# All transposes of an expert visit in one group behind its gate and up products, and the next rows loaded ahead of the last result's store

## The chip, the cores and the metric

One core of a Trainium2 chip runs the whole program. The metric is the device time of one execution in microseconds; the time before is the median of three runs.

## The reference, cut to what is computed

Two decoder layers over 256 positions of width 1024, float32. Layer 0 is a stick-breaking attention with a dense SwiGLU, layer 1 a latent attention (MLA) with a SwiGLU of 8 experts, of which each position takes its best two. The change lies in the experts:

```python
logits = (h @ w_router).astype(jnp.float32) + b_router.astype(jnp.float32)
top_vals, top_idx = lax.top_k(logits, TOP_K)          # TOP_K = 2
top_w = jax.nn.softmax(top_vals, axis=-1)
gates = jnp.sum(jax.nn.one_hot(top_idx, N_EXPERTS, dtype=jnp.float32) * top_w[..., None], axis=-2)
out = jnp.zeros_like(h)
for e in range(N_EXPERTS):                            # 8 experts, 1408 hidden columns each
    out = out + gates[..., e:e + 1] * _swiglu(h, w_gu[e], w_down[e])
```

with `_swiglu(h, w_gu, w_down)` = `(silu(a) * b) @ w_down`, where `a` and `b` are the halves of `h @ w_gu`.

## The kernel before

**Numbers in two parts.** Every product is made of three: each float32 operand is split into a high part that TensorE takes as it is (`F32R`) and a low part, the difference. The product is hi x hi + lo x hi + hi x lo. ScalarE copies a weight piece out of the ring into `m_hi` (`ehi`, L950), VectorE subtracts into `m_lo` (`elo`, L1608). The same is done with activations: `xe_hi`/`xe_lo`, `eT_hi`/`eT_lo`.

**The weight stream.** The sync engine (SP) loads the weights in pieces of at most 1 MB into a ring of six buffers and waits for `freed`, which VectorE counts up with every split, before it fills a buffer again. `m_hi` and `m_lo` have three buffers each (`NB`), so `ehi(k)` waits until TensorE has finished piece k - 3 (`used`).

**A visit.** The positions chosen for an expert are gathered as 128 rows of `x_rows` in DRAM; a visit handles 128 rows of one expert. Here there are 8 visits: the loop `Fori(0, last)` runs seven times with `more=True`, and the last visit is written out behind it with `more=False`. A visit has 18 pieces: 12 of gate and up in three groups j = 0, 1, 2 of 4 pieces (512, 512 and 384 hidden columns, `EW = (4, 4, 3)` blocks of 128), and 6 of the down product, `down(a, g)`, for the output halves a = 0, 1 and the groups g = 0, 1, 2. The gate product of group j is in PSUM bank 2j, the up product in bank 2j + 1, the down products in banks 6 and 7.

**Between gate/up and down.** For each group: ScalarE's `sil(j)` (L1024) takes the Silu of the gate into `esil`; VectorE's `times_up(j)` (L1700) multiplies it with the up product into `ehid[j % 2]`, counted in `e_hid`; TensorE's `turn(j)` (L2386 to L2391) transposes its 4, 4 or 3 blocks with the identity into bank 2j; ScalarE's `eg_hi(j)` (L1028) copies that into `eT_hi`, VectorE's `eg_lo(j)` (L1707) writes the difference to `eT_lo` and counts `e_glo`, for which `down(0, g)` waits. These pieces of work are sewn into the weight splits by hand, in the order that the functions of each engine give.

**Where the transposes stand.** On TensorE, `turn(0)` and `turn(1)` stand in the middle of the gate and up pieces of the following group, `turn(2)` behind `down(0, 0)`. The next visit's input is transposed in two halves, `turn_x` (L2330, four transposes each), behind `down(0, 1)` and `down(0, 2)`, into banks 1 and 3. ScalarE's `x_half` (L997) scales and shifts them into `xe32` and copies to `xe_hi`, VectorE's `x_lo` makes `xe_lo`. The last visit has `turn_sel` (two transposes of the selection matrix) instead.

**The rows in and out.** ScalarE's `y_out` at the start of visit i copies the finished banks 6 and 7 to `ysb` (`e_y`). The GpSimd queue then stores `ysb` to `y_rows`, waits until the store has landed (`s_y`), waits until the last `xe_in` has been transposed (`e_xT`), and loads the next 128 rows into `xe_in` (`s_xe`), L566 to L571. TensorE waits for `s_xe` ahead of its first `turn_x`. So `ysb` is free for the next `y_out` since TensorE got through `s_xe`.

Of the kernel before, what the change touches and what calls it, by code (L numbers as in the profile page):

```python
# [28 lines left out]
P = 128  # L29
# [41 lines left out]
def trunk(nc, x_d, c_d, pos_d, ada_w, ada_b, norm_g, sb_w_in, sb_w_out, mla_w_in, mla_g_q, mla_w_q_up,  # L71
# [83 lines left out]
    with ctx:  # L155
# [137 lines left out]
        eT_hi = sb("eT_hi", [P, EFC, P], F32R, at=base + 20480)  # L293
        eT_lo = sb("eT_lo", [P, EFC, P], F32R, at=base + 26624)
        esil = [sb(f"esil{b}", [P, 512], at=base + 32256 + 2048 * b) for b in range(2)]
        ehid = [sb(f"ehid{b}", [P, 512], at=base + 36352 + 2048 * b) for b in range(2)]
        xT32 = sb("xT32", [P, TC, DC, P], at=base + 36864)
        above = sb("above", [P, TC, E, E], at=acc_at)
        level = sb("level", [P, TC, E, E], at=acc_at + 512)
# [187 lines left out]
        def _(pool):  # L487
# [76 lines left out]
            pool.wait_ge(visit_ok, 1)  # L564
            last = pool.value_load(n_last[0:1, 0:1], min_val=E - 1, max_val=2 * E - 1)
            with pool.Fori(0, last) as i:  # L566
                pool.wait_ge(e_y, i + 1)
                pool.dma_start(y_rows.rearrange("(v p) n -> v p n", p=P)[i], ysb[:, :]).then_inc(s_y, 16)
                pool.wait_ge(s_y, 16 * i + 16)
                pool.wait_ge(e_xT, 2 * i + 2)  # L570
                pool.dma_start(xe_in[:, :], x_rows.rearrange("(v p) n -> v p n", p=P)[i + 1]).then_inc(s_xe, 16)  # L571
            pool.wait_ge(e_y, last + 1)
            pool.dma_start(y_rows.rearrange("(v p) n -> v p n", p=P)[last], ysb[:, :]).then_inc(s_ylast, 16)
            pool.wait_ge(row_ok, 2)
# [12 lines left out]
        def _(act):  # L587
# [431 lines left out]
            def visit_hi(i, more):  # L1019
                def sil(j):  # L1020
                    act.wait_ge(used, M0 + 4 * j + 4 + NK * i)
                    if j >= 2:
                        act.wait_ge(e_hid, EG * i + j - 1)
                    act.activation(esil[j % 2][:, 0:gw[j]], ps[:, 2 * j, 0:gw[j]], ACT.Silu).then_inc(e_sil, 1)  # L1024

                def eg_hi(j):
                    act.wait_ge(e_hidT, EG * i + j + 1)
                    act.activation(eT_hi[:, f0[j]:f0[j] + EW[j], :].rearrange("p a b -> p (a b)"),  # L1028
                                   ps[:, 2 * j, 0:gw[j]], ACT.Copy).then_inc(e_ghi, 1)

                y_out(M0 + NK * i)
                for j in range(EG):
                    ehi(i, 4 * j + 3)
                    if j >= 1:
                        eg_hi(j - 1)
                    ehi(i, 4 * j + 4)
                    ehi(i, 4 * j + 5)
                    sil(j)
                    ehi(i, 4 * j + 6)
                if more:  # L1040
                    eg_hi(EG - 1)
                    ehi(i, NG + 3)
                    x_half(2 * i + 2, 0)
                    ehi(i, NG + 4)
                    ehi(i, NG + 5)
                    ehi(i, NK)
                    x_half(2 * i + 2, 1)
                    for k in range(1, NB):
                        ehi(i, NK + k)
# [13 lines left out]
            with act.Fori(0, last) as i:  # L1063
                visit_hi(i, True)
            visit_hi(last, False)
            act.wait_ge(e_hidT, EG * last + EG)
            act.activation(eT_hi[:, f0[EG - 1]:EFC, :].rearrange("p a b -> p (a b)"),
                           ps[:, 2 * EG - 2, 0:gw[EG - 1]], ACT.Copy).then_inc(e_ghi, 1)
            act.wait_ge(sel_mm, 1)
            act.activation(selT[:, :], ps[:, 1, 0:T], ACT.Copy).then_inc(selT_ok, 1)  # L1070
            act.wait_ge(wt_all, 1)
# [36 lines left out]
        def _(dve):  # L1108
# [588 lines left out]
            def visit_lo(i, more):  # L1697
                def times_up(j):
                    dve.wait_ge(e_sil, EG * i + j + 1)
                    dve.tensor_tensor(ehid[j % 2][:, 0:gw[j]], esil[j % 2][:, 0:gw[j]], ps[:, 2 * j + 1, 0:gw[j]],  # L1700
                                      ALU.mult).then_inc(e_hid, 1)

                def eg_lo(j):
# [4 lines left out]

                for j in range(EG):
                    elo(i, 4 * j + 3)  # L1710
                    if j >= 1:
                        eg_lo(j - 1)
                    elo(i, 4 * j + 4)
                    if j == EG - 1:
                        times_up(j)
                        elo(i, 4 * j + 5)
                        eg_lo(j)
                    else:
                        elo(i, 4 * j + 5)
                        times_up(j)  # L1720
# [67 lines left out]
        def _(pe):  # L1788
# [557 lines left out]
            def visit(i, more):  # L2346
# [39 lines left out]
                def turn(j):  # L2386
                    pe.wait_ge(e_hid, EG * i + j + 1)
                    for a in range(EW[j]):
                        ins = pe.transpose(ps[:, 2 * j, a * P:(a + 1) * P], ehid[j % 2][:, a * P:(a + 1) * P],
                                           ident[:, :])  # L2390
                    ins.then_inc(e_hidT, 1)  # L2391

                pe.wait_ge(e_xhi, 2 * i + 1)
                for j in range(EG):
                    gate_up(4 * j)
                    gate_up(4 * j + 1)
                    if j == 0:
                        pe.wait_ge(e_xlo, 2 * i + 2)
                    if j >= 1:
                        turn(j - 1)  # L2400
                    gate_up(4 * j + 2)
                    gate_up(4 * j + 3)
                pe.wait_ge(e_y, i + 1)
                for g in range(EG):
                    pe.wait_ge(e_glo, EG * i + g + 1)
                    down(0, g)
                    if g == 0:
                        turn(EG - 1)
                        if not more:
                            turn_sel()  # L2410
                    elif more:
                        if g == 1:
                            pe.wait_ge(s_xe, 16 * i + 16)
                        turn_x(2 * i + 2, g - 1)
                for g in range(EG):
                    down(1, g)
                    if g == 1 and not more:
# [82 lines left out]
```

## Time and profile before

| | |
|---|---|
| median of 3 runs | 819.75 us (819.63 to 819.96) |
| the profiled execution | 819.59 us, its span 817.8 us |
| TensorE, matmuls | 794.6 us busy, 97% of the span |
| TensorE, weight loads | 707.0 us, 86% |
| VectorE | 693.9 us, 85% |
| ScalarE | 542.4 us, 66% |
| GpSimd | 48.3 us, 6% |
| chain that ended last | 81% TensorE, 6% VectorE, 4% DMA, 3% ScalarE |
| DMA | 284.31 MB, mean 348 GB/s |

A profile row of the order of time has the start in us from the start of the span, the duration in us of the whole row (from its first start to its last end), the engine (PE is TensorE's matmuls, PEld its weight loads, DVE is VectorE, ACT is ScalarE, POOL is GpSimd), the line of the kernel, what was written and read, and `xN` for N instructions in a row. Matmuls overlap: the one that follows starts before the last has ended, so their cost is the distance between starts and not the duration. A bracket at the end gives how long the engine was idle before the row and who released it.

### The profile page before, as it was taken

The numbers are of one execution on the slowest core, as the hardware profiler recorded it, in microseconds if no ns is written. First come the engines' busy times: TensorE is split into PE (matmuls) and PEld (weight loads), VectorE is DVE, ScalarE is ACT, GpSimd is POOL, SyncE is SP. The second block draws the span as 40 slices with busy tenths as digits, with TensorE's granted clock in tenths as the row PEclk, the third lists the DMA queues.
The fourth block names the chain that finished last, engine by engine and source line by source line (L and its number), as shares of the span: only waits on it lengthen the run. The fifth ranks groups of instructions, "written<-read, shape, count | busy, mean of one in ns | idle before, by whom it ended". The sixth has DMA issues, their size and how long they took to land.

```text
span 817.8 us, 12488 instructions
## 1 busy us (share of the span) xinstructions
PE 794.6 (97%) x4678; PEld 707.0 (86%) x4678; DVE 693.9 (85%) x587; ACT 542.4 (66%) x575; POOL 48.3 (6%) x54
## 2 busy tenths in 40 slices
PE   4999999999999999999999999999999999999995
PEld 4999778999999888999888888888888888888884
DVE  4998797889989886878479898988989898898998
ACT  5447846534344334667388797978788797878875
POOL 1000020020000300000011000000000000000120
PEclk9999999999999999999999999999999999999998
DMA  8999676599999997399929999999999999999992
GB/s 336 422 423 374 247 285 233 187 372 344 357 380 399 355 366 277 132 382 421 421 66 392 426 391 416 351 425 363 399 406 355 412 350 427 359 403 400 359 413 80
DMA packets 46793, 284.31 MB, mean 348 GB/s; under 512 B 6028, under 2 KB 6031, under 8 KB 21156
## 3 DMA queue, kind: packets, MB, share of 16 engines
q1 hardware_dynamic: 41002, 269.06, 83.8%
q0 software_dynamic: 3584, 12.60, 4.0%
q10 hardware_dynamic: 2170, 2.13, 0.8%
q8 instruction: 26, 0.43, 0.2%
q14 instruction: 11, 0.09, 0.0%
HBM read 258.09 MB, written 25.17 MB: 346 GB/s over the span
## 4 chain that ended last, share of the span: by engine, by line
PE 81%; DVE 6%; issue 4%; DMA 4%; ACT 3%; POOL 1%; SPq 0%; DVEq 0%; ACTq 0%; POOLq 0%
PE ps L2367 9%; PE ps L2363 8%; PE ps L2362 8%; PE ps L1855 7%; PE ps L1863 7%; PE ps L1859 7%; PE ps L2378 4%; PE ps L2379 4%; PE ps L2383 4%; PE ps L1791 3%; PE ps L1793 3%; PE ps L1792 3%; DMA ring<-in_ada_w 2%; DVE w_lo L1119 2%; PE ps L1810 1%
## 5 line engine op out<-in xcount | busy, mean ns | idle before, releaser
L1611 DVE TENSOR_TENSOR w_lo<-ring,w_hi 128x2048 fp32r<-128x2048 f32 (+1 forms) x96 | 210.0, 2200 | 29.7 <-ACT w_hi L954 29.4
L608 ACT ACTIVATE w_hi<-ring 128x2048 fp32r<-128x2048 f32 (+1 forms) x56 | 106.4, 1901 | 136.3 <-PE ps L1863 79.9
L954 ACT ACTIVATE w_hi<-ring 128x2048 fp32r<-128x2048 f32 (+1 forms) x96 | 174.8, 1839 | 8.8 <-PE ps L2367 8.8
L1119 DVE TENSOR_TENSOR w_lo<-ring,w_hi 128x2048 fp32r<-128x2048 f32 (+1 forms) x56 | 131.5, 2350 | 33.2 <-ACT w_hi L608 32.7
L1855 PE MATMUL ps<-hT_hi,w_hi 128*128 128x256 f32 x480 | 117.1, 280 | 0.2 <-ACT hT_hi L710 0.2
L1863 PE MATMUL ps<-hT_hi,w_lo 128*128 128x256 f32 x480 | 116.7, 279 | 0.0
L1859 PE MATMUL ps<-hT_lo,w_hi 128*128 128x256 f32 x480 | 116.5, 279 | 0.0
L1611 DVE TENSOR_TENSOR m_lo<-ring,m_hi 128x1536 fp32r<-128x1536 f32 (+1 forms) x48 | 92.7, 1930 | 2.3 <-ACT m_hi L954 1.9
L2363 PE MATMUL ps<-w_hi,xe_lo 128*128 128x512 f32 (+1 forms) x256 | 92.3, 376 | 0.0
L2362 PE MATMUL ps<-w_hi,xe_hi 128*128 128x512 f32 (+1 forms) x224 | 85.1, 380 | 0.0
L1855 PEld LDWEIGHTS ps<-hT_hi,w_hi 128*128 128x128 f32 x480 | 82.5, 188 | 0.5 <-issue 0.4
L1863 PEld LDWEIGHTS ps<-hT_hi,w_lo 128*128 128x128 f32 x480 | 82.6, 188 | 0.0
L1859 PEld LDWEIGHTS ps<-hT_lo,w_hi 128*128 128x128 f32 x480 | 82.4, 187 | 0.0
L954 ACT ACTIVATE m_hi<-ring 128x1536 fp32r<-128x1536 f32 (+1 forms) x48 | 78.0, 1624 | 6.6 <-PE ps L2367 5.6
L1138 DVE SCALAR_TENSOR_TENSOR acc<-ring,cond,acc 128x2048 f32<-128x2048 f32 x28 | 67.4, 2408 | 0.9
L2367 PE MATMUL ps<-w_lo,xe_hi 128*128 128x512 f32 (+1 forms) x256 | 65.2, 376 | 0.1
L2363 PEld LDWEIGHTS ps<-w_hi,xe_lo 128*128 128x128 f32 x256 | 48.1, 188 | 7.3
L2367 PEld LDWEIGHTS ps<-w_lo,xe_hi 128*128 128x128 f32 x256 | 47.2, 188 | 8.1 <-DVE w_lo L1611 0.5
L2378 PE MATMUL ps<-w_hi,eT_hi 128*128 128x512 f32 x128 | 51.4, 402 | 0.0
L2379 PE MATMUL ps<-w_hi,eT_lo 128*128 128x512 f32 x128 | 50.1, 392 | 0.0
L2362 PEld LDWEIGHTS ps<-w_hi,xe_hi 128*128 128x128 f32 x224 | 42.1, 188 | 6.0
L2363 PE MATMUL ps<-m_hi,xe_lo 128*128 128x384 f32 (+1 forms) x128 | 46.5, 363 | 0.0
(407 smaller groups left out, 1464.6 us busy)
## 6 DMA issues: line engine op xcount, KB each, us to landing
ring<-in_moe_w_gu SPq DMA_DIRECT2D x64, 1024.0 KB, 6.7
ring<-in_ada_w SPq DMA_DIRECT2D x48, 1024.0 KB, 7.1
ring<-in_moe_w_down SPq DMA_DIRECT2D x32, 1024.0 KB, 7.4
ring<-in_moe_w_gu SPq DMA_DIRECT2D x32, 768.0 KB, 7.9
ring<-in_ffn_w_gu SPq DMA_DIRECT2D x22, 1024.0 KB, 6.1
ring<-in_sb_w_in SPq DMA_DIRECT2D x12, 1024.0 KB, 9.2
ring<-in_moe_w_down SPq DMA_DIRECT2D x16, 768.0 KB, 6.7
ring<-in_ffn_w_down SPq DMA_DIRECT2D x11, 1024.0 KB, 7.2
```

Of the source, the lines that this page charges most:

```text
L608: act.activation(split_of(m)[0][:, 0:cols_n], ring[n % R][:, 0:cols_n], ACT.Copy).then_inc(hi_done, 1)
L954: act.activation(m_hi[k % NB][:, 0:n_c], ring[(N0 + k) % R][:, 0:n_c], ACT.Copy).then_inc(hi_done, 1)
L1119: dve.tensor_tensor(split_of(m)[1][:, 0:cols_n], ring[n % R][:, 0:cols_n], split_of(m)[0][:, 0:cols_n].bitcast(F32), ALU.subtract).then_in ...
L1611: dve.tensor_tensor(m_lo[k % NB][:, 0:n_c], ring[(N0 + k) % R][:, 0:n_c], m_hi[k % NB][:, 0:n_c].bitcast(F32), ALU.subtract).then_inc(free ...
L1855: return pe.matmul(at(f), bh[:, k, f * P:(f + 1) * P], hT_hi[:, k0 + k, :], start=(begin and k == 0 and f % 2 == 0), stop=False, skip_grou ...
L1859: return pe.matmul(at(f), bh[:, k, f * P:(f + 1) * P], hT_lo[:, k0 + k, :], start=False, stop=stop, skip_group_check=True)
L1863: return pe.matmul(at(f), bl[:, k, f * P:(f + 1) * P], hT_hi[:, k0 + k, :], start=False, stop=stop, skip_group_check=True)
L2362: pe.matmul(o, xe_hi[:, 2 * q + h, :], bh[:, h, s, :], start=q + h == 0, stop=False)
L2363: pe.matmul(o, xe_lo[:, 2 * q + h, :], bh[:, h, s, :], start=False, stop=False)
L2367: ins = pe.matmul(ps[:, 2 * j + s, 0:gw[j]], xe_hi[:, 2 * q + h, :], bl[:, h, s, :], start=False, stop=q == 3 and h == 1)
L2378: pe.matmul(o, eT_hi[:, f, :], bh[:, h, :], start=f == 0, stop=False)
L2379: pe.matmul(o, eT_lo[:, f, :], bh[:, h, :], start=False, stop=False)
```

## The change

On TensorE `turn(0)`, `turn(1)` and `turn(2)` leave their places; behind the last gate and up piece there now stand `turn(0)`, `turn(1)`, the two `turn_x` of the next visit (in the last visit `turn_sel`), and `turn(2)`, and then all down products. For that `ehid` gets a third buffer. ScalarE and VectorE have their three `eg_hi` and `eg_lo` behind `sil(2)` and `times_up(2)`. The GpSimd queue issues the load of the next rows first and the store behind it, and waits for the store no more; TensorE does, ahead of `down(1, 0)`.

```diff
-        ehid = [sb(f"ehid{b}", [P, 512], at=base + 36352 + 2048 * b) for b in range(2)]
+        ehid = [sb(f"ehid{b}", [P, 512], at=base + 36352 + 2048 * b) for b in range(EG)]
...
             with pool.Fori(0, last) as i:
+                pool.wait_ge(e_xT, 2 * i + 2)
+                pool.dma_start(xe_in[:, :], x_rows.rearrange("(v p) n -> v p n", p=P)[i + 1]).then_inc(s_xe, 16)
                 pool.wait_ge(e_y, i + 1)
                 pool.dma_start(y_rows.rearrange("(v p) n -> v p n", p=P)[i], ysb[:, :]).then_inc(s_y, 16)
-                pool.wait_ge(s_y, 16 * i + 16)
-                pool.wait_ge(e_xT, 2 * i + 2)
-                pool.dma_start(xe_in[:, :], x_rows.rearrange("(v p) n -> v p n", p=P)[i + 1]).then_inc(s_xe, 16)
...
                 for j in range(EG):
                     ehi(i, 4 * j + 3)
-                    if j >= 1:
-                        eg_hi(j - 1)
                     ehi(i, 4 * j + 4)
                     ehi(i, 4 * j + 5)
                     sil(j)
+                    if j == EG - 1:
+                        for n in range(EG):
+                            eg_hi(n)
                     ehi(i, 4 * j + 6)
                 if more:
-                    eg_hi(EG - 1)
                     ehi(i, NG + 3)
...
             visit_hi(last, False)
-            act.wait_ge(e_hidT, EG * last + EG)
-            act.activation(eT_hi[:, f0[EG - 1]:EFC, :].rearrange("p a b -> p (a b)"),
-                           ps[:, 2 * EG - 2, 0:gw[EG - 1]], ACT.Copy).then_inc(e_ghi, 1)
...
-                    dve.tensor_tensor(ehid[j % 2][:, 0:gw[j]], esil[j % 2][:, 0:gw[j]], ps[:, 2 * j + 1, 0:gw[j]],
+                    dve.tensor_tensor(ehid[j][:, 0:gw[j]], esil[j % 2][:, 0:gw[j]], ps[:, 2 * j + 1, 0:gw[j]],
...
                 for j in range(EG):
                     elo(i, 4 * j + 3)
-                    if j >= 1:
-                        eg_lo(j - 1)
                     elo(i, 4 * j + 4)
                     if j == EG - 1:
                         times_up(j)
+                        for n in range(EG - 1):
+                            eg_lo(n)
                         elo(i, 4 * j + 5)
                         eg_lo(j)
...
                     gate_up(4 * j + 1)
                     if j == 0:
                         pe.wait_ge(e_xlo, 2 * i + 2)
-                    if j >= 1:
-                        turn(j - 1)
                     gate_up(4 * j + 2)
                     gate_up(4 * j + 3)
+                for j in range(EG - 1):
+                    turn(j)
+                if more:
+                    pe.wait_ge(s_xe, 16 * i + 16)
+                    for b in range(2):
+                        turn_x(2 * i + 2, b)
+                else:
+                    turn_sel()
+                turn(EG - 1)
                 pe.wait_ge(e_y, i + 1)
                 for g in range(EG):
                     pe.wait_ge(e_glo, EG * i + g + 1)
                     down(0, g)
-                    if g == 0:
-                        turn(EG - 1)
-                        if not more:
-                            turn_sel()
-                    elif more:
-                        if g == 1:
-                            pe.wait_ge(s_xe, 16 * i + 16)
-                        turn_x(2 * i + 2, g - 1)
+                if more:
+                    pe.wait_ge(s_y, 16 * i + 16)
                 for g in range(EG):
                     down(1, g)
```

## Rows read from the trace of the kernel before

**Rows 1.** Stretches: us, busy PE, PEld, DVE, ACT, POOL (instructions), granted clock, DMA share, GB/s

```profile
570.30:617.69 47.39, 47.39 (x231) 40.62 (x229) 42.15 (x27) 38.85 (x36) 1.08 (x2) 1.00 0.97 387
15.00:18.00 3.00, 3.00 (x29) 3.00 (x29) 2.86 (x3) 0.60 (x2) 0.00 (x0) 1.00 1.00 419
```

**Rows 2.** Who waited for whom, 440 to 818 us: total us, times, longest

```profile
ACT eT_hi L1028 <- PE ps L2389: 26.8, 23, 1.2
...
POOL xe_in L571 <- DMA y_rows<-ysb: 54.3, 6, 9.3
```

**Rows 3.** Instructions of L2389 and of L2334: count, ns min/median/max, first and last start

```profile
L2389 PE MATMUL ps<-ident,ehid x88: 270/272/275, 444.5 to 793.8; 128*128 128x128 f32 x88
...
L2334 PE MATMUL ps<-ident,xe_in x56: 270/272/275, 465.1 to 752.1; 128*128 128x128 f32 x56
```

**Rows 4.** PE in order of time, visit from 570.3: the pieces' hi x lo matmuls

```profile
582.99 1.07 PE L2367 MATMUL ps<-w_lo,xe_hi 128*128 128x512 f32 x4
...
585.71 1.07 PE L2367 MATMUL ps<-m_lo,xe_hi 128*128 128x512 f32 x4
...
588.92 1.08 PE L2367 MATMUL ps<-w_lo,xe_hi 128*128 128x512 f32 x4
...
596.05 0.86 PE L2367 MATMUL ps<-w_lo,xe_hi 128*128 128x384 f32 x4
...
598.57 0.85 PE L2367 MATMUL ps<-w_lo,xe_hi 128*128 128x384 f32 x4
...
600.65 0.85 PE L2367 MATMUL ps<-m_lo,xe_hi 128*128 128x384 f32 x4
...
603.20 1.08 PE L2383 MATMUL ps<-w_lo,eT_hi 128*128 128x512 f32 x4
...
606.30 1.08 PE L2383 MATMUL ps<-w_lo,eT_hi 128*128 128x512 f32 x4
...
609.04 0.86 PE L2383 MATMUL ps<-m_lo,eT_hi 128*128 128x512 f32 x3
...
612.02 1.07 PE L2383 MATMUL ps<-w_lo,eT_hi 128*128 128x512 f32 x4
```

**Rows 5.** PE in order of time: 16 transposes in a row, layer 0

```profile
15.21 1.91 PE L1918 MATMUL ps<-ident,xhat 128*128 128x128 f32 x16
```

**Rows 6.** PE in order of time, last visit: around turn(2) and turn_sel

```profile
792.66 1.08 PE L2383 MATMUL ps<-w_lo,eT_hi 128*128 128x512 f32 x4
...
795.98 1.07 PE L2383 MATMUL ps<-w_lo,eT_hi 128*128 128x512 f32 x4
```

**Rows 7.** All engines in order of time: turn(1) and what follows; the end of gate/up

```profile
596.74 0.60 PE L2389 MATMUL ps<-ident,ehid 128*128 128x128 f32 x4
...
597.38 0.60 ACT L1028 ACTIVATE eT_hi<-ps 128x512 fp32r<-128x512 f32 x1 [1.03 <-PE ps L2389]
...
598.11 0.68 DVE L1707 TENSOR_TENSOR eT_lo<-ps,eT_hi 128x512 fp32r<-128x512 f32 x1
...
601.54 0.49 ACT L1024 ACTIVATE esil<-ps 128x384 f32<-128x384 f32 x1
...
601.93 1.48 ACT L954 ACTIVATE m_hi<-ring 128x1536 fp32r<-128x1536 f32 x1
...
602.07 0.56 DVE L1700 TENSOR_TENSOR ehid<-esil,ps 128x384 f32<-128x384 f32 x1
```

**Rows 8.** All engines in order of time, tail: TensorE released by ACT and by DVE

```profile
807.52 0.60 ACT L1061 ACTIVATE yl_hi<-ps 128x512 fp32r<-128x512 f32 x1
...
808.26 0.70 PE L2426 MATMUL ps<-yl_hi,selT 128*128 128x512 f32 x2 [0.78 <-ACT yl_hi L1061]
808.43 0.68 DVE L1738 TENSOR_TENSOR yl_lo<-ps,yl_hi 128x512 fp32r<-128x512 f32 x1
...
809.17 0.73 PE L2426 MATMUL ps<-yl_lo,selT 128*128 128x512 f32 x2 [0.21 <-DVE yl_lo L1738]
```

**Rows 9.** POOL in order of time, the same visit: the load of the next rows

```profile
584.57 0.54 POOL L571 DMA_DIRECT2D xe_in<-x_rows  x1 [9.13 <-DMA y_rows<-ysb]
```

More of the change, by code:

```diff
@@ L2388, in turn @@
                     for a in range(EW[j]):
-                        ins = pe.transpose(ps[:, 2 * j, a * P:(a + 1) * P], ehid[j % 2][:, a * P:(a + 1) * P],
+                        ins = pe.transpose(ps[:, 2 * j, a * P:(a + 1) * P], ehid[j][:, a * P:(a + 1) * P],
                                            ident[:, :])
```

## The prediction

> **What bounds the kernel now.** I read the busy shares by stretch first, then the list of waits, then TensorE in order of time. In one expert visit TensorE is busy for 47.39 of 47.39 us, with a granted clock of 1.00, the 16 DMA engines for 0.97 of the time, VectorE for 42.15 and ScalarE for 38.85 us [rows 1]. TensorE is in none of the visits' large waits; those that touch the change are ScalarE's, 26.8 us in 23 waits for the transposes of the hidden rows, and the GpSimd queue's, 54.3 us for the store of the last result [rows 2]. Both are idle time of engines that are not the bound. So only what changes TensorE's own sequence can count. There are 8 visits: 88 transposes at L2389 are 8 x 11, and 56 at L2334 are 7 x 8, since the last visit loads no next rows [rows 3].
>
> **What the transposes cost today.** A piece of 12 matmuls with 512 columns takes 585.71 - 582.99 = 2.72 us, one with 384 columns 600.65 - 598.57 = 2.08, so a matmul 0.227 or 0.173 [rows 4]. The same stretches with a group in them [rows 4]: 588.92 - 585.71 = 3.21, so turn(0) costs 0.49; 598.57 - 596.05 = 2.52, turn(1) 0.44; 606.30 - 603.20 = 3.10, turn(2) 0.38 (three transposes); 609.04 - 606.30 = 2.74 less 10 matmuls, the first half of the next rows 0.47; 612.02 - 609.04 = 2.98 less 11 matmuls, the second half 0.49. Sum: 2.27 us a visit for 19 transposes in five groups. In a long train 16 transposes take 1.91 us, the last of which stands for 0.27, so the pitch is 1.64/15 = 0.109 us [rows 5] and 19 of them are 2.07. The five groups have an overhead of 2.27 - 2.07 = 0.20 us, 0.04 to 0.05 each. That is all that grouping can take off TensorE: four fifths of it, 0.16 a visit, or 0.20 if all goes. The last visit has 11 transposes and two of `sel` in three groups: its first two as above (0.49 and 0.44), the third 795.98 - 792.66 = 3.32 less 2.72 = 0.60 [rows 6]; sum 1.53.
>
> **What the change adds: a chain at the boundary.** Before, the halves of `eT` for group 0 were ready long before the down product; turn(2) even ran behind down(0, 0). Now down(0, 0) waits for turn(0), ScalarE's copy and VectorE's difference, and all of these stand behind the end of gate and up. I count from the moment when TensorE could start the next matmul, 600.65 + 4 x 0.173 = 601.34 [rows 4]. ScalarE starts its Silu at 601.54 (+0.20) and its next work at 601.93 (+0.59); a copy of turned data starts 597.38 - 596.74 = 0.64 after the first transpose of its group. So eg_hi(0) runs from +0.64 for 0.60, to +1.24 [rows 7]. VectorE takes up ScalarE's result 0.04 later (601.54 + 0.49 to 602.07), so at +1.28; but its product for group 2 starts at +0.73 and takes 0.56, to +1.29. eg_lo(0), 0.68, ends at +1.97 [rows 7]. The hand-over to a waiting TensorE is in the trace twice, in the tail: 0.06 us after VectorE (809.11 to 809.17) and 0.14 after ScalarE (808.12 to 808.26); the first matmul after the wait is followed 0.70 - 0.39 = 0.31 later instead of 0.23, so a restart costs 0.08 [rows 8]. Down(0, 0) starts at +2.03 to +2.11. TensorE's own train needs +2.07 to that point, so the wait is nearly hidden; what hides it are the 8 transposes of the next rows, and turn(2) finds its input (+1.29) before its turn at +1.74.
>
> I take +2.11 and one group's overhead, 0.05: 2.16 a visit against 2.27, a gain of 0.11, times 7 visits 0.77 us. In the last visit the 8 transposes are missing, so the cover is thinner: 13 transposes are 1.42, the chain still ends at +2.11, and 2.16 stands against 1.53, a loss of 0.63. It falls in the part from which everything follows to the end. **Sum: -0.14 us.** The profiled execution took 819.59 us (span 817.8 plus 1.8 around it), the median of the runs is 819.75, 0.16 above it; so I forecast 819.6.
>
> **What is moved and costs nothing.**
> - VectorE behind the boundary: after eg_lo(1) its next split (piece 13, 2.29 at the most) runs from about +2.5 to +4.8. Down(0, 1) asks for it 20 matmuls after +2.11, at +6.6. eg_lo(2) then ends at +5.3 and the split of piece 14 at +7.1, asked for at +2.11 + 24 x 0.227 + 6 x 0.227 = +8.9. ScalarE's copy of piece 15 must now wait for down(0, 0), +2.11 + 2.72 + 0.2 = +5.0; it is wanted at +9.6. If this cover were gone, TensorE would wait here in the middle of the down product.
> - The load of the next rows: it moves from behind the store to ahead of it, so that it starts a visit earlier. At present it starts at 584.57, after 9.13 us behind the store [rows 9], and TensorE reads it from 607 on. It wasn't late; the earlier start is worth nothing, but without it the transposes couldn't stand at the boundary (+0.9 is 602). On the GpSimd queue the store stands behind the wait for the transposes of the rows before, which were done in the visit before. Same bytes, same count of DMAs.
> - The store's wait moves to TensorE, ahead of down(1, 0). The store is out by 584.57 - 9.13 = 575.4 and done by 584.6 [rows 9]; down(1, 0) of that visit starts at 612.02 + 4 x 0.227 = 612.9 [rows 4], 28 us later. What would queue behind this wait is all of TensorE.
> - Third buffer for `ehid`, and the copy after the loop taken into the visit: no instruction more. ScalarE's 26.8 us of waits [rows 2] mostly go; nothing waited for them.
>
> **A rule against the change.** Across 16 transposes in a row the granted clock stays 1.00 in the trace [rows 1, 5]. The Trainium skill, "TensorE: Matmul & The Clock Gate", part 4, says that transposes in PE mode don't count as busy for the clock gate. By that rule a train of 19 with a wait behind it could cost clock.
>
> **Rivals.**
> 1. *The boundary wait is dearer than the tail's hand-over* (slower). Now the head of TensorE's queue waits in every visit, with five waits in the train, and the next weight load can't run ahead. It decides from 0.2 us more a visit: 8 x 0.2 on top of 819.6 is 821.2; at 0.25 it is 821.6. For it: the two hand-overs differ by 0.08 already, and the chain has three engines in it. Against: none of the hand-overs read is above 0.14. 0.17.
> 2. *The whole overhead goes* and something with it. Bound by the train alone: 7 x 0.20 = 1.4 off, 2.07 - 1.53 = 0.54 on, 818.9. Should the slow pitch of down(0, 0) (603.20 - 600.65 - 0.69 = 1.86 for 8 matmuls instead of 1.81, [rows 4]) go too, 0.04 x 8 = 0.3 more: 818.6. Only beyond that would it be faster by what can be told. 0.10 for such a result.
> 3. *The clock falls.* A stretch as long as the train, 2.1 us, at 1.2 instead of 2.4 GHz would cost about 2.1 us more each visit, 17 in all: 836. Rows show no fall, and the wait behind the train is short. 0.01.
> 4. *The change does nothing it says*: no group is shorter for standing beside another, since the 0.20 us may belong to the first matmuls after any change of width (down(0, 0) shows 0.04 with no transpose before it). Then a visit pays 2.27 and the chain's +2.11 is covered: 0 for 7 visits, the last one 2.27 - 1.53 = 0.7 on: 820.5. It lies within the 0.72 of no change that can be told.
>
> **Numbers.** Forecast as computed, 0.72, its own range 818.7 to 820.5 (from 7 x 0.20 gained, to rival 4). A change can be told from about 0.2%, 1.6 us. For 8 in 10 I take 818.4, rival 2 and the scatter of the runs, to 821.3, rival 1 at its deciding point. Faster 0.10, same 0.72, slower 0.18.
>
> **What the profile after would show.** TensorE with one train of 19 transposes behind each last gate and up piece, and the first down matmul 2.0 to 2.2 us after it; four stretches of 2.72, 2.08 and 2.72 us where groups were; the visit at about 47.3 instead of 47.39 us; the last visit longer by about 0.6. ScalarE's wait of 26.8 us for transposes down to some 5. Wrong: a wait of TensorE for `eT_lo` of over 0.2 us a visit, a wait of any product in the down part for a split, or a granted clock below 1.00.

## The result: slower by a quarter of a per cent, and the profile after

| | before | after |
|---|---|---|
| median of 10 runs | 819.75 us (819.63 to 820.04) | 821.81 us (821.13 to 822.36) |
| ratio | | 1.0025, interval 1.0017 to 1.0032 |
| profiled execution, its span | 819.59, 817.8 us | 821.46, 819.7 us |

The change costs 2.06 us, outside the range given (818.4 to 821.3), and the runs scatter over 1.2 us where they scattered over 0.4.

The busy times of the page after; no instruction was added or removed on a compute engine, and VectorE's time is the same to a tenth:

```profile
span 819.7 us, 12466 instructions
...
PE 796.5 (97%) x4678; PEld 709.4 (87%) x4678; DVE 693.9 (85%) x587; ACT 544.5 (66%) x575; POOL 46.3 (6%) x54
```

Where the 1.9 us of span went shows in the distances from the first gate matmul of a visit (L2355 before, L2351 after) to that of the next. Three rows of each kernel: its first, second and last visit. Before, TensorE in order of time:

```profile
427.68 1.19 PE L2355 MATMUL ps<-w_hi,xe_hi 128*128 128x512 f32 x4
...
475.57 1.07 PE L2355 MATMUL ps<-w_hi,xe_hi 128*128 128x512 f32 x4
...
759.77 1.07 PE L2355 MATMUL ps<-w_hi,xe_hi 128*128 128x512 f32 x4
```

and after:

```profile
427.93 1.19 PE L2351 MATMUL ps<-w_hi,xe_hi 128*128 128x512 f32 x4
...
476.51 1.07 PE L2351 MATMUL ps<-w_hi,xe_hi 128*128 128x512 f32 x4
...
761.09 1.07 PE L2351 MATMUL ps<-w_hi,xe_hi 128*128 128x512 f32 x4
```

| | before | after | difference | forecast |
|---|---|---|---|---|
| up to the first visit | 427.68 | 427.93 | +0.25 | 0 |
| first visit | 47.89 | 48.58 | +0.69 | -0.11 |
| the six in the middle, each | 47.37 | 47.43 | +0.06, six times 0.38 | -0.11, -0.66 |
| last visit to the end of the span | 58.0 | 58.6 | +0.6 | +0.63 |

The 0.25 us lie ahead of everything that the change touches: one execution's scatter (in the thirteen traces of this document the first visit starts anywhere from 427.54 to 428.36). The last row looks as forecast, but two things are in it, of which one hides part of the other; see below. The same table, made from one execution of each kernel, carries most of what follows; "middle" is the mean of the six.

**The boundary after**, in a middle visit, all engines in order of time (weight loads left out but for one):

```profile
600.77 0.86 PE L2363 MATMUL ps<-m_lo,xe_hi 128*128 128x384 f32 x4
...
601.46 1.04 PE L2385 MATMUL ps<-ident,ehid 128*128 128x128 f32 x8
601.74 0.49 ACT L1023 ACTIVATE esil<-ps 128x384 f32<-128x384 f32 x1 [0.24 <-PE ps L2363]
602.13 1.08 ACT L1027 ACTIVATE eT_hi<-ps 128x512 fp32r<-128x512 f32 x2
...
602.27 0.55 DVE L1696 TENSOR_TENSOR ehid<-esil,ps 128x384 f32<-128x384 f32 x1 [0.52 <-ACT esil L1023]
602.34 1.04 PE L2330 MATMUL ps<-ident,xe_in 128*128 128x128 f32 x8
602.76 1.29 DVE L1703 TENSOR_TENSOR eT_lo<-ps,eT_hi 128x512 fp32r<-128x512 f32 x2
...
603.21 0.49 PE L2385 MATMUL ps<-ident,ehid 128*128 128x128 f32 x3
603.68 0.19 PEld L2374 LDWEIGHTS ps<-w_hi,eT_hi 128*128 128x128 f32 x1 [0.22 <-issue]
603.69 0.49 PE L2374 MATMUL ps<-w_hi,eT_hi 128*128 128x512 f32 x1
...
604.02 0.39 PE L2375 MATMUL ps<-w_hi,eT_lo 128*128 128x512 f32 x1
```

The train is 19 transposes as meant: its first starts at 601.46, its last at 603.21 + 0.49 - 0.27 = 603.43, 1.97 later. The chain is the one described: eT_hi at +0.67 (forecast +0.64), the first eT_lo at +1.30 (forecast +1.29); it takes 0.68 and ends at 603.44, +1.98 (forecast +1.97). But the first down matmul starts at 603.69, **+2.23** and not +2.11: 0.25 us pass between VectorE's end and TensorE's start. In that gap the profile calls TensorE's matmuls busy, since the last transpose runs out at 603.70; only the weight load's row shows idle time. The second matmul follows 0.33 later, where 0.23 is the rule.

**The first visit after**, the same place:

```profile
457.67 1.92 ACT L953 ACTIVATE w_hi<-ring 128x2048 fp32r<-128x2048 f32 x1 [1.13 <-DMA ring<-in_moe_w_down]
458.58 1.03 PE L2385 MATMUL ps<-ident,ehid 128*128 128x128 f32 x8
...
459.49 0.47 ACT L1023 ACTIVATE esil<-ps 128x384 f32<-128x384 f32 x1
...
459.99 0.56 DVE L1696 TENSOR_TENSOR ehid<-esil,ps 128x384 f32<-128x384 f32 x1 [1.12 <-ACT esil L1023]
...
460.60 0.31 PEld L2385 LDWEIGHTS ps<-ident,ehid 128*128 128x128 f32 x3 [0.35 <-DVE ehid L1696]
...
461.41 0.49 PE L2374 MATMUL ps<-w_hi,eT_hi 128*128 128x512 f32 x1 [0.26 <-DVE eT_lo L1703]
```

ScalarE stands 1.13 us before a weight piece from the ring that hasn't landed (piece 13). The Silu of group 2 is queued behind that copy, everything behind the Silu is late, and TensorE waits twice, for `ehid` and for `eT_lo`: the Silu starts 0.91 us after the first transpose and not 0.28, the first down matmul 2.83 us after it and not 2.23. The kernel before has no such wait of ScalarE. Its two copies of pieces 12 and 13 ran in one go, and its Silu came on time:

```profile
455.77 3.72 ACT L954 ACTIVATE w_hi<-ring 128x2048 fp32r<-128x2048 f32 x2
459.44 0.49 ACT L1024 ACTIVATE esil<-ps 128x384 f32<-128x384 f32 x1
```

After the change, the GpSimd queue shows what is new in the first visit:

```profile
445.17 0.58 POOL L568 DMA_DIRECT2D xe_in<-x_rows  x1 [11.57 <-issue]
445.85 0.58 POOL L570 DMA_DIRECT2D y_rows<-ysb  x1
461.22 0.54 POOL L568 DMA_DIRECT2D xe_in<-x_rows  x1 [14.78 <-PE ps L2330]
```

The first load and the first store are issued 0.7 us apart, 1 MB side by side with the ring's pieces in a stretch where the DMA engines are full (from 445 to 458 their busy share is 1.02, at 424 GB/s). In every later visit the load comes at the boundary and the store at the visit's start.

**The last visit.** TensorE's last down piece and its last product, before (for the last product see [rows 8], 809.17) and after:

```profile
806.64 0.84 PE L2383 MATMUL ps<-m_lo,eT_hi 128*128 128x512 f32 x3
```

```profile
808.78 0.84 PE L2379 MATMUL ps<-m_lo,eT_hi 128*128 128x512 f32 x3
...
811.04 0.73 PE L2423 MATMUL ps<-yl_lo,selT 128*128 128x512 f32 x2
```

From the start of the visit the last down piece is at 46.87 before and 47.69 after, 0.82 later; the last product is at 49.40 and 49.95, only 0.55 later. Before, the difference `yl_lo` came 0.91 us after the start of ScalarE's copy (807.52 to 808.43 [rows 8]), behind VectorE's work on the gathered results, and TensorE waited for it; after, it comes 0.64 after the copy (809.66 to 810.30). So a wait at the end took up 0.27 us of what the boundary cost.

Who waited for whom, 440 to 820 us (compare [rows 2]: 26.8 us of ScalarE's waits for the transposes are now 3.6, and nothing is faster for it):

```profile
POOL xe_in L568 <- PE ps L2330: 152.6, 6, 27.6
...
ACT eT_hi L1027 <- PE ps L2385: 3.6, 8, 0.5
```

### The profile page after: what moved, and what is told of

Its sections match the earlier page's. It is cut to its first block, busy times and chain, and to the rows that moved or that the text cites. A ratio compares the mean times of both kernels' runs of the same rounds, so it can differ in the third digit from the quotient of the medians.

```text
span 819.7 us, 12466 instructions
## 1 busy us (share of the span) xinstructions
PE 796.5 (97%) x4678; PEld 709.4 (87%) x4678; DVE 693.9 (85%) x587; ACT 544.5 (66%) x575; POOL 46.3 (6%) x54
## 3 DMA queue, kind: packets, MB, share of 16 engines
q10 hardware_dynamic: 2170, 2.13, 0.8%
## 4 chain that ended last, share of the span: by engine, by line
PE 88%; DVE 6%; ACT 3%; DMA 2%; issue 1%; SPq 0%; DVEq 0%; ACTq 0%
PE ps L2363 10%; PE ps L2359 10%; PE ps L2358 9%; PE ps L1851 7%; PE ps L1855 7%; PE ps L1859 7%; PE ps L2374 5%; PE ps L2375 5%; PE ps L2379 5%; PE ps L1789 3%; PE ps L1787 3%; PE ps L1788 3%; DMA ring<-in_ada_w 2%; DVE w_lo L1115 2%; PE ps L1806 1%
## 5 line engine op out<-in xcount | busy, mean ns | idle before, releaser
L2359 PEld LDWEIGHTS ps<-w_hi,xe_lo 128*128 128x128 f32 x256 | 48.1, 188 | 7.5
L2363 PEld LDWEIGHTS ps<-w_lo,xe_hi 128*128 128x128 f32 x256 | 47.3, 188 | 7.9 <-DVE w_lo L1607 0.5
```

The source lines that it names most:

```text
L2359: pe.matmul(o, xe_lo[:, 2 * q + h, :], bh[:, h, s, :], start=False, stop=False)
L2363: ins = pe.matmul(ps[:, 2 * j + s, 0:gw[j]], xe_hi[:, 2 * q + h, :], bl[:, h, s, :], start=False, stop=q == 3 and h == 1)
```

## The experiments

All runs were timed in five rounds beside the kernel before. Medians of before lay at 819.70 to 819.73. The table gathers them; intervals are with each run. The last three columns come from one profiled execution of each kernel. For kernels 1, 6 and 7 that was the slowest of its runs (828.29, 822.82 and 821.39 us), so their columns show more than the median does.

| kernel | median us | ratio | first | middle | last |
|---|---|---|---|---|---|
| before | 819.75 | | 47.89 | 47.37 | 58.05 |
| changed | 821.81 | 1.0025 | 48.58 | 47.43 | 58.61 |
| 1 old order of the transfers | 825.52 | 1.0069 | 54.65 | 47.43 | 59.20 |
| 2 new order of the transfers alone | 819.65 | 1.0003 | 47.89 | 47.37 | 58.04 |
| 3 hi x hi matmuls first | 819.30 | 0.9996 | 48.11 | 47.19 | 58.04 |
| 4 three more waits | 821.12 | 1.0018 | 48.69 | 47.38 | 58.90 |
| 5 other wait ahead | 820.36 | 1.0010 | 48.62 | 47.30 | 58.44 |
| 6 two more transposes | 821.76 | 1.0025 | 48.53 | 47.43 | 59.99 |
| 7 transfers apart | 820.90 | 1.0013 | 48.18 | 47.41 | 59.14 |
| 8 two groups | 818.87 | 0.9992 | 47.81 | 47.25 | 58.33 |
| 9 Silu first | 820.76 | 1.0013 | 47.95 | 47.43 | 58.64 |
| 10 = 3, 5 and 7 | 818.79 | 0.9991 | 47.76 | 47.18 | 58.20 |
| 11 = 10 and 9 | 819.13 | 0.9994 | 47.77 | 47.19 | 58.63 |

### 1 and 2: the transposes and the transfers, each alone

Kernel 1 is the changed one with the old GpSimd loop and without TensorE's wait for the store; kernel 2 the one before with the new loop and, on TensorE, `pe.wait_ge(s_y, 16 * i + 16)` ahead of `down(1, 0)`:

```diff
-                pool.wait_ge(e_xT, 2 * i + 2)
-                pool.dma_start(xe_in[:, :], x_rows.rearrange("(v p) n -> v p n", p=P)[i + 1]).then_inc(s_xe, 16)
                 pool.wait_ge(e_y, i + 1)
                 pool.dma_start(y_rows.rearrange("(v p) n -> v p n", p=P)[i], ysb[:, :]).then_inc(s_y, 16)
+                pool.wait_ge(s_y, 16 * i + 16)
+                pool.wait_ge(e_xT, 2 * i + 2)
+                pool.dma_start(xe_in[:, :], x_rows.rearrange("(v p) n -> v p n", p=P)[i + 1]).then_inc(s_xe, 16)
```

> The changed kernel with the GpSimd queue's old order (store, wait for it, load of the next rows) and without TensorE's wait for the store. Theory A (two causes: the eT chain at every boundary, and in the first visit the load and the store issued 0.7 us apart, which make a ring piece land late): the first visit falls from 48.58 to 47.95 us, the others stay at 47.43, ratio to before about 1.0017, some 0.6 us below the changed kernel, and its runs scatter less. Rival B (the first visit is long because of the chain alone): no change against the changed kernel, first visit 48.6. Rival C (TensorE's wait for the store is what costs): all visits shorter.

> The kernel before with only the GpSimd queue's new order and TensorE's wait for the store; all transposes where they were. Theory A: a late ring piece in the first visit is covered, since no chain hangs on it: ratio 1.000, visits 47.88 and 47.37 as before. Rival C (the DMA order by itself holds up TensorE): 0.7 us or more slower, in the first visit or through the wait for the store in all of them.

Kernel 2 measured 819.65 us, ratio 1.0003 (0.9994 to 1.0012): but for one run of 11 at 821.50, the transfers' order costs nothing by itself; rival C is out. Kernel 1 went where none of the theories had it: 825.52 us, 1.0069 (1.0055 to 1.0082), in five runs that lie between 823.59 and 828.29. In the profiled one, the slowest, 6.8 of the 8.7 us of span over the kernel before are in the first visit and 1.1 in the last; the visits in the middle are 47.43, as in the changed kernel. TensorE in order of time in the first visit:

```profile
458.75 1.03 PE L2386 MATMUL ps<-ident,ehid 128*128 128x128 f32 x8
...
463.81 1.97 PE L2331 MATMUL ps<-ident,xe_in 128*128 128x128 f32 x8 [4.03 <-DMA xe_in<-x_rows]
...
466.07 0.78 PE L2375 MATMUL ps<-w_hi,eT_hi 128*128 128x512 f32 x1
```

and the stretches around it (busy PE, PEld, DVE, ACT, POOL, then granted clock, DMA share, GB/s):

```profile
455.00:459.00 4.00, 4.00 (x26) 3.97 (x25) 3.29 (x2) 3.63 (x2) 0.59 (x1) 1.00 1.02 427
459.00:465.00 6.00, 1.97 (x14) 1.74 (x12) 4.01 (x5) 1.47 (x3) 0.00 (x0) 0.80 1.02 425
465.00:470.00 5.00, 5.00 (x18) 4.19 (x16) 2.20 (x2) 1.87 (x2) 0.00 (x0) 0.56 0.88 368
470.00:475.00 5.00, 5.00 (x23) 4.13 (x22) 2.51 (x3) 4.31 (x7) 0.00 (x0) 1.00 0.65 220
```

In the first visit the GpSimd queue comes to its loop only at 445, so the rows asked for behind the store land at 463.8, 4 us after the train wants them. In that idle time the granted clock falls from 1.00 to the lower of its two levels, 1.2 GHz: the eight transposes take 1.97 us instead of 1.04. The visit is 6.1 us longer than the changed kernel's in this execution; the medians differ by 3.7. The prediction had called the earlier load "worth nothing" in itself, which kernel 2 bears out, and had judged its need by a middle visit, where the rows are there some 9 us ahead (asked for at 584.57 [rows 9], some 8 us to land, the boundary at 601.3); the one visit in which the order decides is the first. So its sentence that without the new order "the transposes couldn't stand at the boundary" holds for the first visit alone. The Trainium skill, "TensorE: Matmul & The Clock Gate", "HAM oscillation — how this bites in real kernels", says that idle stretches between matmuls send the clock back to half; the trace agrees.

### 3: is it the chain that ends the boundary?

Down(0, 0) first runs its matmuls with `eT_hi`, which wait for `e_ghi` alone:

```diff
-                def down(a, g):
+                def down(a, g, split=False):
...
-                    pe.wait_ge(e_glo, EG * i + g + 1)
-                    down(0, g)
+                    pe.wait_ge(e_ghi if g == 0 else e_glo, EG * i + g + 1)
+                    down(0, g, split=g == 0)
...
+                    if split:
+                        for h in range(EW[g]):
+                            f = f0[g] + h
+                            pe.matmul(o, eT_hi[:, f, :], bh[:, h, :], start=f == 0, stop=False)
+                        pe.wait_ge(e_glo, EG * i + g + 1)
```

> The changed kernel, but down(0, 0) waits for eT_hi alone, runs its four hi x hi matmuls, and waits for eT_lo behind them. Theory A: the chain to the first down matmul is shorter by VectorE's 0.68 us, so it ends ahead of the 19 transposes: the first down matmul 2.0 us after the first transpose instead of 2.22, restart of 0.10 gone, visits 47.43 to about 47.25; in the last visit 0.7 us less; together about 1.8 us below the changed kernel, at or just below the kernel before. Rival B (a train of 19 transposes is slow by itself, or what follows it): visits stay at 47.43.

819.30 us, ratio 0.9996 (0.9987 to 1.0005), 2.5 us below the changed kernel; the middle visits 47.19. The boundary, TensorE's rows:

```profile
600.24 1.03 PE L2391 MATMUL ps<-ident,ehid 128*128 128x128 f32 x8
...
601.12 1.04 PE L2330 MATMUL ps<-ident,xe_in 128*128 128x128 f32 x8
...
601.99 0.49 PE L2391 MATMUL ps<-ident,ehid 128*128 128x128 f32 x3
602.24 1.18 PE L2375 MATMUL ps<-w_hi,eT_hi 128*128 128x512 f32 x4
```

The down product now starts 2.00 us after the first transpose, right behind the last. A train of 19 transposes is not slow by itself, and rival B is out: freed of VectorE's part of the chain, the grouping brings 47.37 - 47.19 = 0.18 us a visit, the size of the overhead worked out (0.20).

### 4, 5 and 6: what the hand-over is made of, and what it hides

Kernel 4 puts three waits that are long satisfied between TensorE's wait for `eT_lo` and `down(0, 0)`; kernel 5 takes the one that stood there away from it; kernel 6 puts two more transposes in each of the seven trains with next rows:

```diff
                     pe.wait_ge(e_glo, EG * i + g + 1)
+                    if g == 0:
+                        pe.wait_ge(e_hid, EG * i + EG)
+                        pe.wait_ge(e_sil, EG * i + EG)
+                        pe.wait_ge(e_ghi, EG * i + 1)
                     down(0, g)
```

```diff
-                def down(a, g):
+                def down(a, g, wait=True):
...
-                    pe.wait_ge(hi_done, M0 + k + 1 + NK * i)
+                    if wait:
+                        pe.wait_ge(hi_done, M0 + k + 1 + NK * i)
...
+                    if g == 0:
+                        pe.wait_ge(hi_done, M0 + NG + 1 + NK * i)
                     pe.wait_ge(e_glo, EG * i + g + 1)
-                    down(0, g)
+                    down(0, g, g > 0)
```

```diff
                     pe.wait_ge(s_xe, 16 * i + 16)
+                    for a in range(2):
+                        pe.transpose(ps[:, 3, a * P:(a + 1) * P], xe_in[:, a * P:(a + 1) * P], ident[:, :])
```

> The changed kernel with three more waits (all long satisfied) between TensorE's wait for eT_lo and the first down matmul. Theory A1 (the hand-over of 0.25 us instead of the 0.06 to 0.14 forecast is made of the waits that stand behind the blocked one): each adds some 0.06 us, so 0.2 us a visit, 1.4 to 1.6 us slower than the changed kernel. Rival A2 (the hand-over is the wake-up of the queue alone, waits behind cost nothing): no change.

> The changed kernel with the wait for piece 12's high part put ahead of the wait for eT_lo, so that no wait stands between the released one and the first down matmul. Waits added behind it cost nothing (47.43 became 47.37 us a visit), so theory A2 (the hand-over of 0.21 to 0.25 us is the wake-up of the queue) expects no change but the few hundredths of a different form: visits 47.35 to 47.45. Rival A1 (the waits behind make it) expects 47.3 and 0.8 us less in all.

> The changed kernel with two more transposes (0.22 us of TensorE, their result unused) in each of the seven trains with next rows. Theory A (the chain eg_hi, eg_lo ends the boundary, TensorE idles 0.2 us behind the train): visits stay within 0.03 us of 47.43, no change in the total. Rival B (TensorE's own train ends it): 0.22 us a visit, 1.5 us slower than the changed kernel. In the first visit, where turn(2) is what TensorE waits for, the two are free by both.

Kernel 6 is the clean one: middle visits 47.43 as before the addition, 821.76 us (ratio 1.0025, 1.0015 to 1.0035) against 821.81. In its trace the first down matmul starts at 603.67, and the train begins at 601.45: +2.22 again. Two transposes, 0.22 us of TensorE, fit into the wait behind the train. (Its last visit holds no added transposes; there ScalarE waits 3.0 us for the ring, in two waits.)

Kernels 4 and 5 gave no simple law. Three more waits made nothing longer; the visit even fell by 0.05 us, to 47.38 (821.12 us, 1.0018, 1.0009 to 1.0027), with 0.21 us from VectorE's end to the first down matmul. With no wait left between the released one and the first weight load the visit fell by 0.13, to 47.30 (820.36 us, 1.0010, 1.0001 to 1.0019), with 0.16 us in that place (the first down matmul at +2.13). The visit is what A1 had expected for that run, though the total fell by 1.45 us and not 0.8, and A1's sum for kernel 4 failed. So the hand-over is not so much per wait. Nor is it fixed by the instructions that stand there: in the first visit of kernel 7, below, the boundary on TensorE is the changed kernel's, and 0.40 us pass. Taking the one wait away brought 0.09 us in the traces; what sets the rest is left open.

### 7 and 9: why the first visit loses most

Kernel 7 issues the store only when the next rows have landed. Kernel 9 leaves the transfers alone and turns ScalarE's order at the boundary, so that the copy of piece 13 no longer stands ahead of the chain:

```diff
                 pool.dma_start(xe_in[:, :], x_rows.rearrange("(v p) n -> v p n", p=P)[i + 1]).then_inc(s_xe, 16)
+                pool.wait_ge(s_xe, 16 * i + 16)
                 pool.wait_ge(e_y, i + 1)
```

```diff
-                    ehi(i, 4 * j + 5)
+                    if j < EG - 1:
+                        ehi(i, 4 * j + 5)
                     sil(j)
                     if j == EG - 1:
-                        for n in range(EG):
+                        for n in range(EG - 1):
                             eg_hi(n)
+                        ehi(i, 4 * j + 5)
+                        eg_hi(EG - 1)
```

> The changed kernel, but the GpSimd queue waits until the next rows have landed before it issues the store. Only the first visit's two transfers are moved apart by that (in the others the rows landed long before). Theory A (load and store side by side make a ring piece late, ScalarE waits 1.1 us for it, and the chain starts late): the first visit from 48.58 to 47.9 to 48.1, the total 0.5 to 0.7 us less, less scatter. Rival (one of the two alone is enough, since the DMA engines are full in that stretch anyway): first visit stays at 48.6.

> The changed kernel, ScalarE's order at the boundary turned: Silu of group 2, eg_hi(0) and eg_hi(1) ahead of the copy of piece 13, for which down(0, 1) asks only 2.7 us later. Theory A (in the first and the last visit piece 13 comes late from the ring, ScalarE stands 1.1 us before it with the Silu behind, and so the whole chain starts late): the first visit from 48.58 to 47.95, the last from 50.29 or more to about 50.1 to 50.2, the other visits at 47.35 to 47.43, total 0.8 to 1.3 us below the changed kernel and little scatter. Rival (the turned order delays the split of piece 13 or eg_lo(2), so that down(0, 1) or down(0, 2) waits): all visits longer by 0.2 us or more.

Kernel 7: 820.90 us, 1.0013 (1.0004 to 1.0022), first visit 48.18, a little above the 47.9 to 48.1 expected. Its rows there, where 1.13 us of waiting for the ring stood:

```profile
456.66 1.92 ACT L954 ACTIVATE w_hi<-ring 128x2048 fp32r<-128x2048 f32 x1 [0.16 <-PE ps L2364]
458.55 1.04 PE L2386 MATMUL ps<-ident,ehid 128*128 128x128 f32 x8
458.83 0.49 ACT L1024 ACTIVATE esil<-ps 128x384 f32<-128x384 f32 x1 [0.24 <-PE ps L2364]
```

The Silu starts 0.28 us after the first transpose, as in a middle visit, instead of 0.91. What keeps the visit above 47.95 is the hand-over of 0.40 us named above (VectorE ends at 460.52, the first down matmul starts at 460.92).

Kernel 9: 820.76 us, 1.0013 (1.0004 to 1.0022), and its 11 runs lie within 0.56 us (820.34 to 820.90). A wait for the ring is still there, now for piece 12 and well ahead of the boundary; piece 13 is copied behind the chain's first copies, without a wait:

```profile
454.83 1.92 ACT L953 ACTIVATE w_hi<-ring 128x2048 fp32r<-128x2048 f32 x1 [1.03 <-DMA ring<-in_moe_w_down]
...
458.35 1.03 PE L2388 MATMUL ps<-ident,ehid 128*128 128x128 f32 x8
458.63 0.49 ACT L1023 ACTIVATE esil<-ps 128x384 f32<-128x384 f32 x1 [1.89 <-PE ps L2366]
...
459.98 1.93 ACT L953 ACTIVATE w_hi<-ring 128x2048 fp32r<-128x2048 f32 x1
```

The first visit is 47.95, to the hundredth what was expected, and the middle ones stay at 47.43, so the later copy of piece 13 holds up nothing. The last visit, which was to get shorter too, did not (58.64). Two different repairs, one of the transfer and one of the order behind it, take 0.4 and 0.6 us off the same visit: the late piece and the chain behind it cost together, neither by itself (kernel 2 has the same transfers and no chain, at 47.89). The trace of kernel 7 has its own late piece in the last visit, 1.1 us, and that visit reads 59.14; such waits of ScalarE in the last visit stand in the traces of 1, 3 to 8 and 10 (0.4 to 3.0 us), and not in those of before, of the changed kernel, of 2, 9 and 11. That they come from the gathers of the last results, which run at that time, was not tried.

### 8, 10 and 11: versions that keep the gain

Kernel 8 groups without the chain: `turn(0)` and `turn(1)` together in the middle of group 2's pieces, `turn(2)` and the next rows together behind `down(0, 0)`, with the copies and differences moved to match:

```diff
+                    if j == EG - 1:
+                        for n in range(EG - 1):
+                            turn(n)
                     gate_up(4 * j + 2)
...
                     down(0, g)
+                    if g == 0:
+                        turn(EG - 1)
+                        if more:
+                            pe.wait_ge(s_xe, 16 * i + 16)
+                            for b in range(2):
+                                turn_x(2 * i + 2, b)
+                        else:
+                            turn_sel()
```

> The changed kernel with its transposes in two groups: turn(0) and turn(1) in the middle of group 2's gate and up pieces, turn(2) and the next rows (or the selection) behind down(0, 0), with ScalarE's and VectorE's work moved to match. No chain ends at the boundary, and three groups fewer than before. Theory A (each group beyond the first has an overhead of 0.04 to 0.06 us, nothing else is lost): visits 47.2, first visit 47.75, last visit as before; total 1.0 to 1.3 us below the kernel before, ratio 0.9985. Rival (the overhead does not belong to the groups): visits 47.37 as before, ratio 1.000. Rival 2 (two copies and two differences in a row hold up the weight splits): TensorE waits for a split in group 2, slower than before.

818.87 us, ratio 0.9992 (0.9983 to 1.0001), middle visits 47.25: three groups fewer are 0.12 us, 0.04 each, as read from [rows 4] and [rows 5]. The two other rivals are out. The total fell by 0.9 us where 1.0 to 1.3 were expected: the last visit is 0.28 longer than before, with a wait of TensorE of 0.4 us for `yl_lo` at its end where the kernel before has 0.21. The gain is real in the visits; the total's interval just touches no change.

> The changed kernel with three repairs seen to count: down(0, 0) starts with its hi x hi matmuls behind eT_hi alone, the wait for piece 12 stands ahead of that wait, and the store waits until the next rows have landed. Theory A: visits 47.19 or a little less, first visit 47.8 to 47.9, last visit 49.7 with some scatter from the ring; total 818.5 to 818.9, ratio to before 0.9987. Rival (the parts don't add up, since turn(2)'s wait for ehid takes over where the chain ends earlier): first visit stays at 48.1, total 819.3 as with the hi matmuls alone.

> As the run before, and with ScalarE's Silu ahead of the copy of piece 13. Theory A: the first visit 47.7, the last 49.6, the others 47.19: total 818.2 to 818.6, ratio about 0.9983, the fastest of the forms with one train. Rival (the late copy of piece 13 is felt in the down product now that nothing else is slack): visits above 47.3, no gain over the run before.

Kernel 10 has the edits of 3, 5 and 7 (the wait for piece 12 ahead of that for `eT_hi`): 818.79 us, 0.9991 (0.9982 to 1.0000), level with kernel 8, 0.9 us below before and 3.0 below the changed kernel. Its first visit is 47.76, so the parts add up. Kernel 11 adds the edit of 9: 819.13 us, 0.9994 (0.9985 to 1.0003), no gain over 10 where 818.2 to 818.6 had been expected, and the rival's sign, visits above 47.3, didn't show either. Its visits are the same; what it loses in the profiled execution is in the last visit (58.63). There TensorE's last down piece is 0.15 us earlier in the visit than in kernel 10 (47.14 against 47.29), but the last product then waits for `yl_lo`:

```profile
808.44 0.73 PE L2436 MATMUL ps<-yl_lo,selT 128*128 128x512 f32 x2 [0.43 <-DVE yl_lo L1738]
```

As in the kernel before, `yl_lo` stands behind VectorE's work on the gathered results. In kernel 10 TensorE's matmuls show no such wait. From 8, 11 and before it looks as if a second path, over ScalarE, VectorE and the gathers, ends the last visit once TensorE is early enough; no run was made to test that.

## Why the prediction was wrong

- **What bounds the kernel: right.** TensorE; ScalarE got back 23 us of waits and the kernel slowed down. What changed in the time shows as waits and distances in TensorE's rows, except at the end of the last visit.
- **The overhead of the groups, 0.20 us a visit: right.** Kernel 3 shows 0.18 for four groups fewer, kernel 8 0.12 for three, so rival 4 (groups no shorter side by side) is out.
- **The chain at the boundary: the right chain, to 0.02 us up to VectorE's end; the hand-over was mis-sized.** The sum took 0.14 us for it, from the tail, and 0.05 for one group's overhead; the restart of 0.08 that it had read in the tail is no term of its own. Measured: 0.25 for the hand-over, and the first down matmul is followed 0.33 us later instead of 0.23, 0.10 more. The visit was to fall by 0.11 and grew by 0.06. That is six times 0.17, 1.0 us, half of the error. This was one of the prediction's own signs of being wrong: a wait for `eT_lo` of over 0.2 us a visit. The sum of [rows 4], 2.27, also left out 0.04 us at down(0, 0), named but not counted, and 0.03 where 512 columns change to 384; the second stays in the changed kernel and moves nothing.
- **The cover: right up to VectorE's end.** "What hides it are the 8 transposes of the next rows" is so: the last transpose starts at +1.97, the chain ends at +1.98. The hand-over behind it stays open, and kernel 6 fits two more transposes into it.
- **The first visit was read as one of the seven.** This is the step that failed altogether. All rows came from a middle visit, where the load goes out at the boundary. In the first, GpSimd comes late to its loop, so that load and store are issued together, the ring's piece 13 is 1.1 us late, and it stands ahead of the Silu in ScalarE's queue. Forecast -0.11, measured +0.69; of the 0.80 between them 0.17 is the hand-over as in the other visits, the rest the late Silu (kernel 9 takes 0.63 off). The kernel before copied the same piece at about 457.6, the second half of its merged row, and didn't feel it: its boundary came at 459.44 - 0.20 = 459.24, 0.7 us later than the changed kernel's at 458.58 and 0.9 later counted from the visit's start, since eight transposes lay ahead of it, and nothing at the boundary waited for the Silu. "Costs nothing" for the new order of the transfers named the wrong visit as its cover.
- **The last visit: +0.63 forecast, +0.6 measured, but by luck.** The boundary cost 0.82 us there, 0.19 more than forecast, the same mis-sized hand-over as in every visit (the first down matmul 2.25 us after the first transpose, and 0.33 to the next). 0.27 us of it vanished in a wait for `yl_lo` at the end that the kernel before had and the prediction did not count.
- **The rivals.** The result lies on rival 1's side, whose mechanism held at 0.17 us a visit over the forecast, just under the 0.2 from which it was to decide; the rest is the late piece that none of them had. Rival 2 (the whole overhead goes) needed a boundary without the hand-over, as in kernel 3. Rival 3 fell: with 19 transposes and the wait behind them the granted clock stays at 1.00,

```profile
571.36:618.79 47.43, 47.43 (x230) 40.83 (x229) 42.10 (x27) 39.09 (x36) 1.06 (x2) 1.00 1.00 393
```

so the rule of the Trainium skill ("TensorE: Matmul & The Clock Gate", part 4) that transposes don't count as busy cost nothing here. Kernel 1's drop followed on 4 us with no work at all.

## What to carry to other kernels

Grouping small pieces of work on the bound engine saves a few hundredths of a microsecond for each group, and a chain over three engines that ends at a point where the bound engine can do nothing else costs more: move work together only where its results are wanted later, or let the part of the consumer go first that needs the shortest part of the chain. The hand-over from VectorE to a waiting TensorE took 0.25 us in the middle visits here, and the restart 0.1: don't count with the best case of the trace. And read the first and the last round of a loop by themselves: queues start there from another state, and a copy that waits for the ring must not stand ahead of the chain's first link.

## What the runs showed of the hardware

- The same kind of hand-over has several prices: from VectorE's end to TensorE's start 0.06 us in the tail [rows 8], 0.05 for the third `turn` of the first visit (460.55 to 460.60), 0.25 for the down product of a middle visit, 0.21 with three more satisfied waits there, 0.16 with none, and 0.40 in the first visit of kernel 7.
- ScalarE's Silu at a boundary began 0.04 us after the last matmul's end before, straight behind a copy (601.50 to 601.54), and 0.11 after the change, where ScalarE had been idle for 0.24 us (601.63 to 601.74), with the same wait.
- In kernel 1, after 4 us without work, TensorE's granted clock was 0.56 on the average of the stretch from 465 to 470, in which it was busy throughout, and 1.00 from 470 to 475.
